# Seven of eight chunks of the experts' gate and up as split products, the down weights' high part in a place of its own

## The chip, the core and the metric

The kernel runs as one program on one core of a Trainium2 chip. The metric is the device time of one execution in microseconds (us); lower is better. The five engines are named as in the profile: PE (TensorE, matrix products; PEld is its weight load), DVE (VectorE), ACT (ScalarE), POOL (GpSimd) and SP (SyncE, which issues most of the DMA transfers).

## The reference

One inference step of a one-layer decoder for 512 prompt tokens and 8 sample tokens, all in float32: a mixing layer (pooling heads and an RG-LRU recurrence), cross-attention to a memory, and a mixture of experts. The change is in the experts alone. There are 64 routed experts of width 256, each token goes to 8 of them, and a shared expert is added:

```python
def body(acc, blk):
    tok, wt, e = blk
    xb = h_pad[tok]
    a = jax.nn.silu(xb @ w_gate[e]) * (xb @ w_up[e])
    yb = (a @ w_down[e]).astype(jnp.float32) * wt[:, None]
    return acc.at[tok].add(yb), None
```

Each expert has `w_gate` and `w_up` of 1024 x 256 and `w_down` of 256 x 1024, 1 MB each. So one pass over the experts reads 3 MB of weights for each of them, beside the tokens' rows.

## The kernel before

All stages ahead of the experts (mixing, attention, routing, shared expert) are as they were, and the change leaves them alone but for places in memory. After some 440 us the expert loop begins. It works on blocks of 96 slots (`SLOTS`), each with the tokens of one expert; there are 64 blocks in this execution, numbered here from 0. The first four (`step_of_block(0, j, peeled=True)`) are written out; the others run in a hardware loop with four blocks a turn (`RING = 4`).

For block b, in the order of PE's instruction stream (`step_of_block` in the tensor program):

- `slots(b + 2)`: five tiny products (L1868) that turn the routing table into the row numbers of block b + 2.
- `gate_up_whole` (L1933): the contraction over D = 1024 is cut into `KD = 8` chunks of 128. The first `WHOLE_K = 2` chunks are multiplied as whole float32, from the raw weights `WG` and the raw tokens `hX`. One such product of 96 tokens by 512 columns (gate and up side by side) is two MATMUL instructions in the trace, called passes below.
- `gate_up(.., 0)` and `gate_up(.., 1)` (L1920): the other six chunks as split products, three chunks in each half. A number is written as a high part (rounded to the PE's one-pass format fp32r) and a low part (the rest), and a product is high*high + low*high + high*low: three MATMULs a chunk.
- `turn_act(b - 1)` (L1940) turns the activations of the block before.
- `turn(b + 1)` (L1905) turns the gathered tokens of the next block, eight transposes into PSUM `pair[1]`.
- `down(b - 1)` (L1954): the down product of the block before as twelve split MATMULs.

ACT makes the high parts by a cast: `cut_up` (L992) in two halves of 1536 elements for gate and up, `cut_down` (L1027) for the 2048 of down, `turn` (L1017 copies the whole chunks to `hX`, L1018 casts the others to `h_parts`), `at` for the activations; it also does the `silu` (L1013) and scales the result (`down`, L1032). DVE subtracts to get the low parts: `cut_up` (L1455), `cut_down` (L1505), `turn` (L1495), `at` (L1509); it does the `gate` product (L1500) and makes the slots' tables (L1342 to L1351).

SP loads the weights into a ring of four sets. `load_up` for block b + 4 (L600 gate, L601 up) waits until `gate_up` of block b is done; `load_down` (L606) until `down` is done. Both loads of `load_up` count on one semaphore, `wg_in`, and ACT's `cut_up(.., 0)` waits for both. POOL gathers the tokens' rows (L706) and adds the results to `acc_rows` in memory (`scatter`, L715). Before the loop it also writes the shared expert's result to `acc_rows` (L724) from `rows`, five transfers, and waits until they have landed (`sums_landed`).

In memory, the high parts of gate and up have two places in `w_hi` (even and odd blocks), 3072 columns each; the high part of down, `WD_hi`, lies between them, in the same 8192 columns.

Of the kernel before, what the change touches and what calls it, by code (L numbers as in the profile page):

```python
# [28 lines left out]
NTT = len(TILES)  # L29
# [7 lines left out]
FE, KF = 256, 2  # L37
# [7 lines left out]
SLOTS = 96  # L45
WHOLE_K = 2
CUT_K = (KD - WHOLE_K) // 2
CUT = CUT_K * 256
RING = 4
# [173 lines left out]
def trunk(nc, x_prompt, x_sample, state_pool, state_conv, state_h, cache_mem_k, cache_mem_v, mem_prompt, norm_mix,  # L223
# [5 lines left out]
    with ExitStack() as ctx:  # L229
# [7 lines left out]

        with nc.sbuf_tensor("w_hi", [P, 8192], F32R) as w_hi:
            pass
# [23 lines left out]
        with nc.sbuf_tensor("unused_L5", [P, 10872], F32), nc.sbuf_tensor("shared_parts", [P, 2, KF, NT], F32R) as shared_parts:  # L263
            pass
        with nc.sbuf_tensor("unused_L3", [P, 10872], F32), nc.sbuf_tensor("h_parts", [P, 2, 2, CUT_K * SLOTS], F32R) as h_parts:
            pass
# [132 lines left out]
        gath = [view(regL, 8824 + D * j, D) for j in range(PAIR)]  # L399
        hX = view(regL, 12024, WHOLE_K, SLOTS)  # L400
        places = view(regL, 14200, 112)
# [6 lines left out]
        WD_lo = [view(lo_A, 4096, KF, D), view(lo_A, 10240, KF, D), view(lo_B, 4096, KF, D), view(lo_B, 6144, KF, D)]  # L408
        WG_hi = [view(w_hi, 5120, 2, 2, CUT), view(w_hi, 0, 2, 2, CUT)]
        last_hi = view(w_hi, 5120, KF, D)  # L410
        sdw_hi, sdw_lo = WD_lo[3], view(lo_C, 4096, KF, D)
        WD_hi = view(w_hi, 3072, KF, D)

# [330 lines left out]
        def _(a):  # L744
# [242 lines left out]
            def cut_up(r, b, q, half):  # L987

                if half == 0:
                    a.wait_ge(wg_in[r], q * 32 + 32)  # L990
                k0 = WHOLE_K + half * CUT_K
                a.copy(WG_hi[r % 2][:, half], WG[r][:, :, k0 * FE:(k0 + CUT_K) * FE]).then_inc(wg_hi, 1)  # L992

# [81 lines left out]
        def _(v):  # L1075
# [375 lines left out]
            def cut_up(r, b, half):  # L1451
                v.wait_ge(wg_hi, 2 * b + half + 1)
                k0 = WHOLE_K + half * CUT_K
                cols = slice(k0 * FE, (k0 + CUT_K) * FE)
                v.tensor_tensor(WG_lo[r][:, :, cols], WG[r][:, :, cols], WG_hi[r % 2][:, half].bitcast(F32),  # L1455
                                ALU.subtract).then_inc(wg_lo, 1)
# [36 lines left out]
            def turn(b):  # L1493
                v.wait_ge(turned_a, b + 1)
                v.tensor_tensor(h_parts[:, 1], pair[1][:, :, SLOTS:(1 + CUT_K) * SLOTS], h_parts[:, 0].bitcast(F32),  # L1495
                                ALU.subtract).then_inc(turned_d, 1)
# [55 lines left out]
        def _(pe):  # L1552
# [344 lines left out]
            def turn(g, b, q, first=False):  # L1897

                pe.wait_ge(gath_in[g], q * 16 + 16)
                if not first:  # L1900
                    pe.wait_ge(turned_d, b)
                g3 = gath[g].rearrange("p (f k) -> p k f", k=KD)
                for k in range(KD):
                    h, n = (k, 0) if k < WHOLE_K else ((k - WHOLE_K) // CUT_K, 1 + (k - WHOLE_K) % CUT_K)
                    ins = pe.transpose(pair[1][:, h, n * SLOTS:(n + 1) * SLOTS], g3[0:SLOTS, k, :], ident[0:SLOTS, 0:SLOTS])  # L1905
                ins.then_inc(turned, 1)

            def gate_up(r, b, half):

                out = pair[0][0:SLOTS, 0, :].rearrange("p (s f) -> p s f", s=2)  # L1910
                hi = WG_hi[r % 2][:, half].rearrange("p s (k f) -> p s k f", k=CUT_K)
                lo = WG_lo[r].rearrange("p s (k f) -> p s k f", k=KD)
                pe.wait_ge(wg_lo, 2 * b + half + 1)
                if half == 0:
                    pe.wait_ge(turned_d, b + 1)
                for k in range(CUT_K):
                    kk = half * CUT_K + k
                    x_hi, x_lo = (h_parts[:, x, half, k * SLOTS:(k + 1) * SLOTS] for x in range(2))
                    for s, (x, w) in enumerate(((x_hi, hi[:, :, k, :]), (x_lo, hi[:, :, k, :]), (x_hi, lo[:, :, WHOLE_K + kk, :]))):
                        ins = pe.matmul(out, x, w, start=False, stop=half == 1 and k == CUT_K - 1 and s == 2,  # L1920
                                        skip_group_check=True)
                if half == 1:
                    ins.then_inc(gu_made, 1)

            def gate_up_whole(r, b, q, first=False):
# [87 lines left out]
```

## Time and profile before

| | |
|---|---|
| time, three executions | 1109.17, 1110.92, 1112.01 us (median 1110.92) |
| the profiled execution | 1109.17 us, its span 1107.4 us |
| PE busy | 1061.4 us, 96% of the span |
| DVE, ACT, POOL busy | 748.3, 646.5, 262.8 us |
| moved by DMA | 299 MB, 270 GB/s over the span |
| granted TensorE clock | 0.982 of full speed over the execution |

The span is what the profiler saw between the first and the last instruction; 1.8 us of the profiled time lie around it. PE's busy time holds overlapping instructions, so it says that PE is nearly always at work, not that it is at its peak. What a stage is bound by is read from the chain of work and from the waits.

### The profile page before, as it was taken

How to read it: one execution, taken by the hardware profiler on the slowest of the kernel's cores; microseconds unless marked ns; L12 is line 12 of the kernel's file. 1: busy time of each engine (PE TensorE's matmuls, PEld its weight loads, DVE VectorE, ACT ScalarE, POOL GpSimd, SP SyncE). 2: the span in 40 equal slices, each digit the busy share in tenths (PEclk: the TensorE clock that was granted, in tenths of full speed). 3: DMA queues.
4: the chain of work that ended last, by engine and by line, in shares of the span. 5: the costliest groups of instructions: out<-in, count | busy, mean ns of one | idle time of the engine just before them, and what ended most of it. 6: DMA issues, size and time to landing. Idle time of an engine off the chain costs nothing.

```text
span 1107.4 us, 17623 instructions
## 1 busy us (share of the span) xinstructions
PE 1061.4 (96%) x5991; PEld 796.5 (72%) x5991; DVE 748.3 (68%) x1332; ACT 646.5 (58%) x850; POOL 262.8 (24%) x180
## 2 busy tenths in 40 slices
PE   5999999999999999999999999999999999999991
PEld 5999458999669888666667666766667666766660
DVE  4733834633934575787788777887788778887762
ACT  4374343432643313677767776677767776677662
POOL 1001320000000101233333333333333333333321
PEclk8999999999999899999999999999999999999996
DMA  9500336050953525899999999999999999999945
GB/s 300 225 4 31 142 143 229 1 229 27 379 211 157 227 79 192 288 359 375 368 367 369 368 377 363 351 357 357 364 366 369 359 356 358 369 367 374 361 113 172
DMA packets 64342, 299.02 MB, mean 270 GB/s; under 512 B 12591, under 2 KB 15227, under 8 KB 39718
## 3 DMA queue, kind: packets, MB, share of 16 engines
q1 hardware_dynamic: 49102, 261.93, 61.7%
q0 software_dynamic: 15200, 36.55, 13.4%
q8 instruction: 26, 0.43, 0.2%
q14 instruction: 14, 0.11, 0.0%
HBM read 281.34 MB, written 34.00 MB: 285 GB/s over the span
## 4 chain that ended last, share of the span: by engine, by line
PE 90%; DMA 3%; DVE 3%; ACT 2%; SPq 1%; issue 1%; POOLq 0%; ACTq 0%; DVEq 0%
PE pair L1920 23%; PE pair L181 18%; PE pair L1954 16%; PE pair L1933 10%; PE pair L1659 5%; PE pair L1905 5%; PE pair L1562 3%; PE pair L1940 1%; DMA regA<-in_w_in 1%; PE pS L1868 1%; PE pair L1752 1%; PE pair L1760 1%; PE pS L1731 1%; DMA acc_rows<-regL 1%; DMA regL<-h_rows,regL 1%; DVE regL L1113 1%
## 5 line engine op out<-in xcount | busy, mean ns | idle before, releaser
L1920 PE MATMUL pair<-w_hi,h_parts 128*96 128x512 f32 x768 | 267.7, 430 | 0.0
L715 POOL DMA_INDIRECT acc_rows<-regL x64 | 93.0, 1453 | 389.8 <-ACT regL L1032 275.2
L1920 PEld LDWEIGHTS pair<-w_hi,h_parts 128*96 128x96 f32 x768 | 121.5, 165 | 69.7 <-issue 33.9
L1954 PE MATMUL pair<-w_hi,act_parts 128*96 128x512 f32 x512 | 165.0, 404 | 2.6 <-DVE act_parts L1509 2.6
L706 POOL DMA_INDIRECT regL<-h_rows,regL x65 | 139.7, 2148 | 74.7 <-DVE regL L1351 49.4
L1032 ACT ACTIVATE regL<-pair,regL 96x1024 f32<-96x1024 f32 x64 | 71.1, 1110 | 125.0 <-PE pair L1954 125.0
L1455 DVE TENSOR_TENSOR lo_A<-regA,w_hi 128x1536 fp32r<-128x1536 f32 x64 | 111.9, 1749 | 0.2 <-ACT w_hi L992 0.2
L1954 PEld LDWEIGHTS pair<-w_hi,act_parts 128*96 128x96 f32 x512 | 80.2, 167 | 29.9 <-issue 2.8
L992 ACT CAST w_hi<-regA 128x1536 fp32r<-128x1536 f32 x64 | 94.7, 1482 | 0.0
L1505 DVE TENSOR_TENSOR lo_B<-regB,w_hi 128x2048 fp32r<-128x2048 f32 x32 | 73.4, 2293 | 29.6 <-ACT w_hi L1027 29.6
L1505 DVE TENSOR_TENSOR lo_A<-regA,w_hi 128x2048 fp32r<-128x2048 f32 x32 | 73.4, 2292 | 24.7 <-ACT w_hi L1027 24.7
L1342 DVE SCALAR_TENSOR_TENSOR regL<-regL 128x480 bf16<-128x480 f32 x66 | 47.4, 719 | 49.3 <-issue 49.3
L181 PE MATMUL pair<-h_hi,win_parts 128*128 128x260 f32 x384 | 71.4, 288 | 5.9 <-DVE h_lo L1107 5.9
L1920 PE MATMUL pair<-lo_A,h_parts 128*96 128x512 f32 x192 | 75.4, 393 | 0.0
L1905 PEld LDWEIGHTS pair<-ident,regL 96*128 96x128 f32 x520 | 67.8, 201 | 8.8 <-DMA regL<-h_rows,regL 1.3
L1905 PE MATMUL pair<-ident,regL 96*128 96x96 f32 x520 | 66.7, 271 | 1.1 <-DMA regL<-h_rows,regL 0.8
L181 PEld LDWEIGHTS pair<-h_hi,win_parts 128*128 128x128 f32 x384 | 60.1, 192 | 6.9 <-issue 5.1
L1933 PE MATMUL pair<-regA,regL 128*96 128x512 f32 x128 | 61.9, 606 | 0.8 <-ACT h_parts L1018 0.8
L1027 ACT CAST w_hi<-regA 128x2048 fp32r<-128x2048 f32 x32 | 60.5, 1891 | 0.0
L1027 ACT CAST w_hi<-regB 128x2048 fp32r<-128x2048 f32 x32 | 60.5, 1890 | 0.0
L1455 DVE TENSOR_TENSOR lo_C<-regC,w_hi 128x1536 fp32r<-128x1536 f32 x32 | 56.0, 1749 | 0.0
L1455 DVE TENSOR_TENSOR lo_B<-regB,w_hi 128x1536 fp32r<-128x1536 f32 x32 | 55.9, 1748 | 0.0
(344 smaller groups left out, 2207.3 us busy)
## 6 DMA issues: line engine op xcount, KB each, us to landing
regA<-in_exp_w_gate SPq DMA_DIRECT2D x32, 1024.0 KB, 9.1
regA<-in_exp_w_up SPq DMA_DIRECT2D x32, 1024.0 KB, 12.2
regA<-in_exp_w_down SPq DMA_DIRECT2D x32, 1024.0 KB, 14.0
regB<-in_exp_w_down SPq DMA_DIRECT2D x32, 1024.0 KB, 15.3
regB<-in_exp_w_gate SPq DMA_DIRECT2D x16, 1024.0 KB, 10.0
regB<-in_exp_w_up SPq DMA_DIRECT2D x16, 1024.0 KB, 13.6
regC<-in_exp_w_gate SPq DMA_DIRECT2D x16, 1024.0 KB, 9.2
regC<-in_exp_w_up SPq DMA_DIRECT2D x16, 1024.0 KB, 12.6
```

Of the source, the lines that this page charges most:

```text
L181: ins = pe.matmul(pair[p][:, h, 0:HALF], w, x[:, k, cols], start=u % 2 == 0 and j == 0 and i == 0, stop=u % 2 == 1 and j == HALF_K - 1 and ...
L706: pool.indirect_dma_start(gath[g][0:SLOTS, :], None, h_rows, bass.IndirectOffsetOnAxis(ap=sums[0:SLOTS, r, 0:1].bitcast(U32), axis=0), bou ...
L715: pool.indirect_dma_start(acc_rows, bass.IndirectOffsetOnAxis(ap=kept[0:SLOTS, r, 0:1].bitcast(U32), axis=0), yX[r][0:SLOTS, :], None, bou ...
L992: a.copy(WG_hi[r % 2][:, half], WG[r][:, :, k0 * FE:(k0 + CUT_K) * FE]).then_inc(wg_hi, 1)
L1027: a.copy(hi, WD[r]).then_inc(wd_hi, 1)
L1032: a.activation(yX[r][0:SLOTS, :].rearrange("p (h n) -> p h n", h=2), pair[2][0:SLOTS, :, :], ACT.Copy, scale=kept[0:SLOTS, r, 1:2]).then_i ...
L1455: v.tensor_tensor(WG_lo[r][:, :, cols], WG[r][:, :, cols], WG_hi[r % 2][:, half].bitcast(F32), ALU.subtract).then_inc(wg_lo, 1)
L1505: v.tensor_tensor(WD_lo[r], WD[r], hi.bitcast(F32), ALU.subtract).then_inc(wd_lo, 1)
L1905: ins = pe.transpose(pair[1][:, h, n * SLOTS:(n + 1) * SLOTS], g3[0:SLOTS, k, :], ident[0:SLOTS, 0:SLOTS])
L1920: ins = pe.matmul(out, x, w, start=False, stop=half == 1 and k == CUT_K - 1 and s == 2, skip_group_check=True)
L1933: pe.matmul(pair[0][0:SLOTS, 0, :].rearrange("p (s f) -> p s f", s=2), hX[:, k, :], w[:, :, k, :], start=k == 0, stop=False, skip_group_ch ...
L1954: ins = pe.matmul(pair[2][0:SLOTS, h, :], act_parts[:, x, k, :], w[:, k, cols], start=k == 0 and s == 0, stop=k == KF - 1 and s == 2)
```

## The change

`WHOLE_K` goes from 2 to 1: one chunk is multiplied whole, seven are split. The halves become three chunks (1 to 3) and four chunks (4 to 7). The high parts of seven chunks need 3584 columns for each of the two places, and `w_hi` grows to 8320 columns that these two fill; the down weights' high part `WD_hi` moves to `wd_parts`, a place over the first part of the region that holds `rows` before the loop. So that the transfers which still read `rows` are done before ACT writes there, ACT now waits for `sums_landed` once, ahead of its step for block 1.

```diff
-WHOLE_K = 2
-CUT_K = (KD - WHOLE_K) // 2
-CUT = CUT_K * 256
+WHOLE_K = 1
+CUT_KS = (range(WHOLE_K, KD // 2), range(KD // 2, KD))
+CUT = (KD - WHOLE_K) * 256
...
-        with nc.sbuf_tensor("w_hi", [P, 8192], F32R) as w_hi:
+        with nc.sbuf_tensor("w_hi", [P, 8320], F32R) as w_hi:
...
+        with nc.sbuf_tensor("unused_L4", [P, 4160], F32), nc.sbuf_tensor("wd_parts", [P, KF * D], F32R) as wd_parts:
...
-        WD_hi = view(w_hi, 3072, KF, D)
+        WD_hi = view(wd_parts, 0, KF, D)
...
-                a.copy(hX[:, :, :], pair[1][:, :, 0:SLOTS])
-                a.copy(h_parts[:, 0], pair[1][:, :, SLOTS:(1 + CUT_K) * SLOTS]).then_inc(turned_a, 1)
+                a.copy(hX, pair[1][:, 0, 0:SLOTS])
+                a.copy(h_parts[:, 0], pair[1][:, :, 0:KD // 2 * SLOTS]).then_inc(turned_a, 1)
...
             for t in range(NTT):
                 start_sums(t)
+            a.wait_ge(sums_landed, 16 * NTT)
...
-                for k in range(CUT_K):
-                    kk = half * CUT_K + k
+                for k in CUT_KS[half]:
+                    n = k % (KD // 2)
```

On PE, in the products of the first block, the kernel before has two whole products ahead of its split ones (`regA` and `regL` are raw weights and raw tokens, `w_hi` the weights' high part, `lo_A` their low part):

```order
L1933 MATMUL pair<-regA,regL 96x512 [waits turned_a,wg_in0]
L1933 MATMUL pair<-regA,regL 96x512
L1920 MATMUL pair<-w_hi,h_parts 96x512 [waits turned_d,wg_lo]
L1920 MATMUL pair<-w_hi,h_parts 96x512
L1920 MATMUL pair<-lo_A,h_parts 96x512
```

and the same place of the change:

```order
L1936 MATMUL pair<-regA,regL 96x512 [waits turned_a,wg_in0]
L1923 MATMUL pair<-w_hi,h_parts 96x512 [waits turned_d,wg_lo]
L1923 MATMUL pair<-w_hi,h_parts 96x512
L1923 MATMUL pair<-lo_A,h_parts 96x512
L1923 MATMUL pair<-w_hi,h_parts 96x512 x2
```

One whole product a block has gone, and the split ones wait for the tokens' low part (`turned_d`) one product sooner; three split products more stand at the end of the second half (12 in place of 9). On ACT, at the entry of the loop (the copies of the shared expert's rows, then block 1), the kernel before has:

```order
L1002 COPY regL<-pair 128x1024 [waits made] x4
L1002 COPY regL<-pair 8x1024 [waits made]
L992 CAST w_hi<-regA 128x1536 [waits wg_in1]
L992 CAST w_hi<-regA 128x1536
L1013 ACTIVATE regL<-pair 96x256 [waits gu_made]
L1017 COPY regL<-pair 128x192 [waits turned]
L1018 CAST h_parts<-pair 128x576
L1027 CAST w_hi<-regA 128x2048 [waits wd_in0]
```

and the change:

```order
L1004 COPY regL<-pair 128x1024 [waits made] x4
L1004 COPY regL<-pair 8x1024 [waits made]
L994 CAST w_hi<-regA 128x2x768 [waits wg_in1,sums_landed]
L994 CAST w_hi<-regA 128x2x1024
L1015 ACTIVATE regL<-pair 96x256 [waits gu_made]
L1019 COPY regL<-pair 128x96 [waits turned]
L1020 CAST h_parts<-pair 128x768
L1029 CAST wd_parts<-regA 128x2048 [waits wd_in0]
```

The order of the instructions is the same; the cast for block 1 now stands behind the landing of the rows, the second cast is a third longer, and so is the cast of the tokens. On DVE, in the step of one block, the kernel before has:

```order
L1505 TENSOR_TENSOR lo_A<-regA,w_hi 128x2048 [waits wd_hi]
L1509 TENSOR_TENSOR act_parts<-pair,act_parts 128x192 [waits at_hi]
L1455 TENSOR_TENSOR lo_B<-regB,w_hi 128x2x768 [waits wg_hi]
L1500 TENSOR_TENSOR regL<-regL,pair 96x256 [waits silu_b]
L1455 TENSOR_TENSOR lo_B<-regB,w_hi 128x2x768 [waits wg_hi]
L1495 TENSOR_TENSOR h_parts<-pair,h_parts 128x576 [waits turned_a]
```

and the change:

```order
L1508 TENSOR_TENSOR lo_A<-regA,wd_parts 128x2048 [waits wd_hi]
L1512 TENSOR_TENSOR act_parts<-pair,act_parts 128x192 [waits at_hi]
L1457 TENSOR_TENSOR lo_B<-regB,w_hi 128x2x768 [waits wg_hi]
L1503 TENSOR_TENSOR regL<-regL,pair 96x256 [waits silu_b]
L1457 TENSOR_TENSOR lo_B<-regB,w_hi 128x2x1024 [waits wg_hi]
L1498 TENSOR_TENSOR h_parts<-pair,h_parts 128x768 [waits turned_a]
```

Nothing has changed places; the last two subtractions are a third longer.

## Rows read from the trace of the kernel before

**Rows 1.** The page: engines' busy time, then the chain's shares.

```profile
PE 1061.4 (96%) x5991; PEld 796.5 (72%) x5991; DVE 748.3 (68%) x1332; ACT 646.5 (58%) x850; POOL 262.8 (24%) x180
...
PE 90%; DMA 3%; DVE 3%; ACT 2%; SPq 1%; issue 1%; POOLq 0%; ACTq 0%; DVEq 0%
```

**Rows 2.** Chain of work, from 690 us: start, us, what.

```profile
689.97 1.29 PE pair L1933 x3
691.25 2.07 PE pair L1920 x9
...
699.43 1.80 PE pair L1933 x4
701.23 0.46 PE pair L1920 x2
```

**Rows 3.** Stretches: engines' busy us (instructions), clock, DMA share, GB/s.

```profile
480.00:680.00 200.00, 200.00 (x983) 137.40 (x983) 161.77 (x222) 144.53 (x161) 73.45 (x40) 1.00 1.02 370
680.00:780.00 100.00, 100.00 (x492) 68.57 (x491) 80.72 (x110) 72.27 (x81) 36.45 (x20) 1.00 1.02 357
...
880.00:980.00 100.00, 100.00 (x493) 68.68 (x491) 80.96 (x111) 72.28 (x81) 36.52 (x20) 1.00 1.02 360
...
610.00:620.00 10.00, 10.00 (x51) 6.87 (x50) 8.10 (x12) 7.22 (x9) 3.68 (x2) 1.00 1.00 349
...
680.00:690.00 10.00, 10.00 (x50) 6.86 (x49) 8.07 (x11) 7.23 (x9) 3.65 (x2) 1.00 0.99 357
```

**Rows 4.** DMA issues at 676, 965 and 1035 us: last column us to landing.

```profile
regC<-in_exp_w_up SPq DMA_DIRECT2D x1, 1024.0 KB, 8.2
...
regA<-in_exp_w_up SPq DMA_DIRECT2D x1, 1024.0 KB, 25.6
...
regC<-in_exp_w_up SPq DMA_DIRECT2D x1, 1024.0 KB, 24.7
```

**Rows 5.** Timeline and chain of block 63's load, casts and products.

```profile
1035.29 0.38 SPq L601 DMA_DIRECT2D regC<-in_exp_w_up  x1
...
1061.12 1.49 ACT L992 CAST w_hi<-regC 128x1536 fp32r<-128x1536 f32 x1
...
1064.65 0.38 ACT L1013 ACTIVATE regL<-pair 96x256 f32<-96x256 f32 x1 [0.38 <-PE pair L1920]
...
1069.31 1.89 ACT L1027 CAST w_hi<-regB 128x2048 fp32r<-128x2048 f32 x1
...
1068.44 1.80 PE pair L1933 x4
```

**Rows 6.** Timeline of DVE in one block.

```profile
702.22 2.29 DVE L1505 TENSOR_TENSOR lo_A<-regA,w_hi 128x2048 fp32r<-128x2048 f32 x1 [0.80 <-ACT w_hi L1027]
...
706.36 0.41 DVE L1500 TENSOR_TENSOR regL<-regL,pair 96x256 f32<-96x256 f32 x1
706.69 1.75 DVE L1455 TENSOR_TENSOR lo_C<-regC,w_hi 128x1536 fp32r<-128x1536 f32 x1
708.36 0.75 DVE L1495 TENSOR_TENSOR h_parts<-pair,h_parts 128x576 fp32r<-128x576 f32 x1
709.44 0.16 DVE L1348 TENSOR_REDUCE regL<-pS 96x2 f32<-96x6 f32 x1 [0.33 <-PE pS L1868]
```

**Rows 7.** Timelines of ACT, POOL and PE where the loop begins.

```profile
441.71 2.85 ACT L992 CAST w_hi<-regA 128x1536 fp32r<-128x1536 f32 x2
...
447.42 1.04 POOL L706 DMA_INDIRECT regL<-h_rows,regL  x1 [4.80 <-DMA acc_rows<-regL]
...
459.94 1.94 PE L1933 MATMUL pair<-regB,regL 128*96 128x512 f32 x4
```

**Rows 8.** SP's issues after the loop's start, and the first one's landing.

```profile
460.07 0.33 SPq L606 DMA_DIRECT2D regA<-in_exp_w_down  x1
466.39 0.33 SPq L600 DMA_DIRECT2D regB<-in_exp_w_gate  x1
...
regA<-in_exp_w_down SPq DMA_DIRECT2D x1, 1024.0 KB, 6.3
```

More of the change, by code:

```diff
@@ L264, in trunk @@
             pass
-        with nc.sbuf_tensor("unused_L3", [P, 10872], F32), nc.sbuf_tensor("h_parts", [P, 2, 2, CUT_K * SLOTS], F32R) as h_parts:
+        with nc.sbuf_tensor("unused_L4", [P, 4160], F32), nc.sbuf_tensor("wd_parts", [P, KF * D], F32R) as wd_parts:
+            pass
+        with nc.sbuf_tensor("unused_L3", [P, 10872], F32), nc.sbuf_tensor("h_parts", [P, 2, 2, KD // 2 * SLOTS], F32R) as h_parts:
             pass
@@ L399, in trunk @@
         gath = [view(regL, 8824 + D * j, D) for j in range(PAIR)]
-        hX = view(regL, 12024, WHOLE_K, SLOTS)
+        hX = view(regL, 12408, SLOTS)
         places = view(regL, 14200, 112)
@@ L408, in trunk @@
         WD_lo = [view(lo_A, 4096, KF, D), view(lo_A, 10240, KF, D), view(lo_B, 4096, KF, D), view(lo_B, 6144, KF, D)]
-        WG_hi = [view(w_hi, 5120, 2, 2, CUT), view(w_hi, 0, 2, 2, CUT)]
-        last_hi = view(w_hi, 5120, KF, D)
+        WG_hi = [view(w_hi, 4160, 2, CUT), view(w_hi, 0, 2, CUT)]
+        last_hi = view(w_hi, 4160, KF, D)
         sdw_hi, sdw_lo = WD_lo[3], view(lo_C, 4096, KF, D)
-        WD_hi = view(w_hi, 3072, KF, D)
+        WD_hi = view(wd_parts, 0, KF, D)
         yf = view(regA, 0, NTT, D)
@@ L990, in cut_up @@
                     a.wait_ge(wg_in[r], q * 32 + 32)
-                k0 = WHOLE_K + half * CUT_K
-                a.copy(WG_hi[r % 2][:, half], WG[r][:, :, k0 * FE:(k0 + CUT_K) * FE]).then_inc(wg_hi, 1)
+                lo, hi = CUT_KS[half][0] * FE, (CUT_KS[half][-1] + 1) * FE
+                a.copy(WG_hi[r % 2][:, :, lo - WHOLE_K * FE:hi - WHOLE_K * FE], WG[r][:, :, lo:hi]).then_inc(wg_hi, 1)
             for half in range(2):
@@ L1452, in cut_up @@
                 v.wait_ge(wg_hi, 2 * b + half + 1)
-                k0 = WHOLE_K + half * CUT_K
-                cols = slice(k0 * FE, (k0 + CUT_K) * FE)
-                v.tensor_tensor(WG_lo[r][:, :, cols], WG[r][:, :, cols], WG_hi[r % 2][:, half].bitcast(F32),
+                lo, hi = CUT_KS[half][0] * FE, (CUT_KS[half][-1] + 1) * FE
+                v.tensor_tensor(WG_lo[r][:, :, lo:hi], WG[r][:, :, lo:hi],
+                                WG_hi[r % 2][:, :, lo - WHOLE_K * FE:hi - WHOLE_K * FE].bitcast(F32),
                                 ALU.subtract).then_inc(wg_lo, 1)
@@ L1494, in turn @@
                 v.wait_ge(turned_a, b + 1)
-                v.tensor_tensor(h_parts[:, 1], pair[1][:, :, SLOTS:(1 + CUT_K) * SLOTS], h_parts[:, 0].bitcast(F32),
+                v.tensor_tensor(h_parts[:, 1], pair[1][:, :, 0:KD // 2 * SLOTS], h_parts[:, 0].bitcast(F32),
                                 ALU.subtract).then_inc(turned_d, 1)
@@ L1903, in turn @@
                 for k in range(KD):
-                    h, n = (k, 0) if k < WHOLE_K else ((k - WHOLE_K) // CUT_K, 1 + (k - WHOLE_K) % CUT_K)
+                    h, n = k // (KD // 2), k % (KD // 2)
                     ins = pe.transpose(pair[1][:, h, n * SLOTS:(n + 1) * SLOTS], g3[0:SLOTS, k, :], ident[0:SLOTS, 0:SLOTS])
@@ L1910, in gate_up @@
                 out = pair[0][0:SLOTS, 0, :].rearrange("p (s f) -> p s f", s=2)
-                hi = WG_hi[r % 2][:, half].rearrange("p s (k f) -> p s k f", k=CUT_K)
+                hi = WG_hi[r % 2].rearrange("p s (k f) -> p s k f", k=KD - WHOLE_K)
                 lo = WG_lo[r].rearrange("p s (k f) -> p s k f", k=KD)
@@ L1915, in gate_up @@
                     pe.wait_ge(turned_d, b + 1)
-                for k in range(CUT_K):
-                    kk = half * CUT_K + k
-                    x_hi, x_lo = (h_parts[:, x, half, k * SLOTS:(k + 1) * SLOTS] for x in range(2))
-                    for s, (x, w) in enumerate(((x_hi, hi[:, :, k, :]), (x_lo, hi[:, :, k, :]), (x_hi, lo[:, :, WHOLE_K + kk, :]))):
-                        ins = pe.matmul(out, x, w, start=False, stop=half == 1 and k == CUT_K - 1 and s == 2,
+                for k in CUT_KS[half]:
+                    n = k % (KD // 2)
+                    x_hi, x_lo = (h_parts[:, x, half, n * SLOTS:(n + 1) * SLOTS] for x in range(2))
+                    for s, (x, w) in enumerate(((x_hi, hi[:, :, k - WHOLE_K, :]), (x_lo, hi[:, :, k - WHOLE_K, :]), (x_hi, lo[:, :, k, :]))):
+                        ins = pe.matmul(out, x, w, start=False, stop=k == KD - 1 and s == 2,
                                         skip_group_check=True)
@@ L1932, in gate_up_whole @@
                 for k in range(WHOLE_K):
-                    pe.matmul(pair[0][0:SLOTS, 0, :].rearrange("p (s f) -> p s f", s=2), hX[:, k, :], w[:, :, k, :],
+                    pe.matmul(pair[0][0:SLOTS, 0, :].rearrange("p (s f) -> p s f", s=2), hX, w[:, :, k, :],
                               start=k == 0, stop=False, skip_group_check=True)
```

## The prediction, made before the change was run

> **What bounds the kernel now.** I read the page first: PE is busy 96% of the span and the chain that ended last runs through PE for 90% of it [rows 1]. That makes PE the bound of the average, so the next view is the chain inside the expert loop, where the change lies. There it is PE alone: from the first split product of one block (691.25 us) to that of the next (701.23) are 9.98 us without a gap [rows 2], and the stretches show PE busy for all of their time [rows 3]. So a PE that does less per block gains at once, if nothing else is as near to its limit. Two things are.
>
> The first is DMA. In the same stretches the mean share of the 16 engines is 1.02, which means that transfers lie one over the other the whole time, and what they move is 370 GB/s up to 680 us, then 357 and 360 [rows 3]. A block needs what 370 GB/s brought in 9.98 us while the loads kept up: 3.69 MB. At 357 to 360 GB/s that takes 10.25 to 10.34 us, longer than PE's block. The landings show it: the last load of a set landed 8.2 us after its issue at 676 us, and 25.6 us after it at 965 us [rows 4]. That is 17.4 us lost over 29 blocks, 0.6 us a block for the slowest of the engines that share a load. PE does not feel it before the end only because the ring of four sets is a reserve, and this reserve is spent: block 63's up weights are issued at 1035.29 and land 24.7 us later, at 1059.99 [rows 4, 5]; ACT's cast of them starts at 1061.12, 1.13 us after that [rows 5].
>
> The second is DVE, whose idle time in a block is 0.80 us before the down weights' subtraction and 0.33 us before the next block's first slot instruction [rows 6], beside an issue gap that stays.
>
> **The change, part by part.** *PE.* Three whole passes take 1.29 us, so one is 0.43 and a chunk (two) 0.86; nine split products take 2.07 us, so one is 0.23 and a chunk (three) 0.69 [rows 2]. A block gets 0.86 - 0.69 = 0.17 us shorter, 9.81 us; for 64 blocks that is 10.9 us.
>
> *ACT and DVE.* The second cast of a block goes from 1.49 to 1.89 us (the down cast has 2048 elements, as it will have) [rows 5]; its subtraction goes from 1.75 to 2.29 us, and the tokens' subtraction from 0.75 to about 0.95 us (576 to 768 elements, at the (2.29 - 1.75)/512 ns per element of the other) [rows 6]. On DVE that is 0.74 us more and a period 0.17 us shorter, 0.91 us, against 1.13 us of waits. It fits with 0.2 us to spare and is costed at nothing. If that cover went, every 0.1 us over would cost 6 us in 62 blocks. ACT's 0.6 us more is of no account; its busy share is 58% [rows 1].
>
> *The wait for the rows, once.* ACT starts the casts for block 1 at 441.71 now. The transfers for which it will wait release POOL's gather at 447.42 [rows 7], so the casts start at about 447.4. Behind the wait stand, on ACT, both casts (1.49 + 1.89) and the silu (0.38) [rows 5], then on DVE the gate (0.41), the longer subtraction (2.29) and the tokens' (0.95) [rows 6]: 7.4 us, and block 1's split products can start at 454.8. The rest of that block is 9.81 - 0.86 = 8.95 us, so block 2 begins at 463.7 where it begins at 459.94 now [rows 7]: 3.8 us later. (PE loses some of that now, in waits at the same place; they are inside the 459.94.)
>
> *The new place of the down weights' high part* costs no instruction; its casts and products keep their sizes. *The smaller copy to hX* is shorter and hidden.
>
> *Where the 0.17 us a block goes.* A faster PE asks for 3.69 MB in 9.81 us, 376 GB/s, more than any long stretch shows [rows 3]. The loads can't come faster, so in the last part of the loop PE waits for them, and the end is set by when block 63's weights land, not by PE's sum. That landing moves only with idle time of the DMA engines. Some comes in at the start: at 466.39 SP issues block 6's loads, and the one before it (issued at 460.07, landed 6.3 us later) lands at 466.4 [rows 8]. There was nothing in stock, so issues that come 3.8 us later leave the engines idle by up to 3.8 us, and all later landings shift by it. Some is won back: the share falls below 1.02 at a few places, 1.00 at 610 us and 0.99 at 680 [rows 3], where a PE ahead of its old pace would have loads waiting; two such stretches hold 0.5 us of idle time, and a few more may add up to 2 us. I call the shift s; its bounds are 0 and 3.8, and I take 2.
>
> From the landing to block 63's first split product the chain is now 1070.24 - 1061.12 = 9.1 us long (1068.44 + 1.80 is that product's start) [rows 5], because PE is late, not ACT. When the loads are late it shrinks to its work: casts and silu 1.49 + 1.89 + 0.38, then 0.41 + 2.29 + 0.95 on DVE, 7.4 us as above. Behind it the second half has three products more, 0.69 us. So the end moves by s - 1.13 - (9.1 - 7.4) + 0.69 = s - 2.1: with s = 2 by -0.1 us, with the bounds by -2.1 to +1.7. Against the profiled execution's 1109.17 (span 1107.4 and 1.8 around it) that is 1109.1, bounds 1107.1 to 1110.9.
>
> The profiled execution is the lowest of three, the others took 1110.92 and 1112.01. PE never waited in the loop of the one that is shown, so I think that in the others late loads had already used up the 1.13 us and the compressible part of the 9.1. By the shorter pieces of now (1.49 twice, 0.38, 0.41, 1.75, 0.75) the chain's least is 6.3 us. In such an execution the change adds s + (7.4 - 6.3) + 0.69 = s + 1.8: 3.8 us with s = 2, bounds 1.8 and 5.6. On 1110.92 that is 1114.7. That the spread comes from there is a guess, so I take a value between the two sums (1109.1 and 1114.7), 1111.5 us: no change that a measurement could tell. For this kernel three executions lie within 0.3%, which I take as about what can be told from no change: below 1107.6 is faster, above 1114.3 slower.
>
> Here two figures of the Trainium skill stand against each other. "DMA: Bandwidth & Descriptors" (Specifications) gives about 358 GB/s of HBM per core, and the late stretches' 357 and 360 agree; by it alone 3.69 MB would take 10.3 us, and this is the forecast. "HBM Reference" (Specifications) says that a core streaming alone measures about 425 GB/s, by which the set would take 8.7 us (an estimate from that page) and DMA would leave PE free; no stretch here shows it beside the gathers and the scatters.
>
> **The rivals.** *PE stays the bound to the end.* Block 2 starts 3.8 us late and 62 blocks win 0.17 each: 3.8 - 10.5 = -6.7, or 1102.5 us against the profiled execution, 1104 against the median. For it speaks that up to 680 us the loads kept pace at 370 GB/s with landings of 8.2 us [rows 3, 4], so that the slow stretches might be a chance of this execution; against it, that they make up most of the loop's second half, and that even 370 is under 376.
>
> *The start's delay is paid in full and nothing is won back (the other side).* The place is ACT's wait at 441.71. With s = 3.8 and loads that bind already, +5.6 us: 1116.5. It decides from s = 1.5 on, where s + 1.8 passes the 3.3 us that can be told. For it: no stock of loads at 466 us [rows 8]. Against it: the profiled execution had 1.13 us and 1.7 us of slack before it.
>
> *DVE becomes the bound.* If its 0.2 us of reserve is not there (a hand-over between ACT and DVE that the sum leaves out), the loop's period is its own, 9.9 or 10 us. As the loads already ask for 10.1 or more in the second half, this adds little to the forecast and would only take away the first rival's gain. It is counted with the forecast.
>
> **How the numbers follow.** Chances: the forecast (loads bind, the start costs some, times of 1107 to 1114.5) 0.60; PE the bound, 1102 to 1105, 0.17; the delay in full, 1114.5 to 1117, 0.23. The range takes in the forecast, the upper half of the first rival and most of the second: 1104 to 1116.5. Faster 0.18, same 0.58, slower 0.24 come from these, with a little of the forecast beyond each bound.
>
> **What would show it.** PE's block in the middle of the loop is 9.81 us (wrong if it is 9.98: a step on DVE or the products is mispriced). Block 2 starts near 463.7, with ACT's cast for block 1 near 447.4 behind the landing of the rows. In the loop's second half PE shows gaps that ACT's first cast ends, with DMA named as what is waited for, and block 63's up weights land within 2 us of 1062. The share of DMA stays at 1.02 and the rate at 355 to 370 GB/s. The prediction is wrong if the rate rises to 376 with PE's share at full to the end (the first rival), or if DVE has no idle time left before 680 us.

## The result, and the profile after

The changed kernel takes 1132.68 us (median of four, 1127.46 to 1136.80) against 1110.05 (1108.87 to 1112.01): a ratio of 1.0195, with a 95% interval of 1.0171 to 1.0219. The forecast was 1111.5 in a range of 1104 to 1116.5, so it was 21 us off, and the time lies above the range's upper end. Ratios in this document leave out executions that are over 1.5% above the fastest of the same kernel, so for a kernel whose times spread they differ from the ratio of the medians.

The profiled execution has 1132.45 us and a span of 1130.7. Its page, to be put beside [rows 1]:

```profile
PE 1064.8 (94%) x6055; PEld 804.2 (71%) x6055; DVE 792.2 (70%) x1332; ACT 667.6 (59%) x850; POOL 262.6 (23%) x180
...
DMA 49%; PE 40%; issue 4%; DVE 3%; ACT 2%; SPq 1%; POOLq 1%; POOL 0%; ACTq 0%; DVEq 0%
```

PE's busy time hardly moved, and DVE's grew by 44 us, about what its longer subtractions ask for; but the chain that ended last is another: PE's 90% of it became 40%, and 49% is DMA now. In the loop that chain is one kind of transfer after another (start, us, what):

```profile
591.98 10.10 DMA acc_rows<-regL
...
602.97 8.98 DMA acc_rows<-regL
...
612.87 9.74 DMA acc_rows<-regL
...
623.50 9.24 DMA acc_rows<-regL
```

These are the scatters that add a block's result to `acc_rows`. Each must wait until the one ahead has landed (`sums_landed`), and none of the eight groups of rows ahead of the prediction looks at them. The waits from 480 to 1080 us (total, times, longest) say the same, and that PE now waits for the gathered tokens:

```profile
POOL acc_rows L717 <- DMA acc_rows<-regL: 358.3, 56, 6.9
...
PEld pair L1908 <- DMA regL<-h_rows,regL: 36.2, 45, 1.6
...
PE pair L1908 <- DMA regL<-h_rows,regL: 17.5, 29, 1.2
```

Over the same stretch of the kernel before, the scatter's longest wait is for its own sums:

```profile
POOL acc_rows L715 <- ACT regL L1032: 245.6, 41, 6.0
```

The stretches that answer to [rows 3]:

```profile
480.00:680.00 200.00, 194.53 (x977) 135.57 (x976) 171.36 (x214) 146.64 (x158) 74.02 (x39) 1.00 1.02 358
680.00:780.00 100.00, 97.03 (x483) 66.58 (x481) 84.32 (x109) 73.24 (x77) 34.21 (x19) 1.00 1.02 354
880.00:980.00 100.00, 95.82 (x480) 66.45 (x479) 83.78 (x106) 72.78 (x79) 35.57 (x20) 1.00 1.02 353
```

PE is no longer busy all the time. The DMA share is 1.02 as before at a lower rate, and yet the loads are in good time: block 63's up weights are issued at 1061.19, land 10.6 us later and are cast at 1086.97, 15 us after that (in [rows 5] the slack was 1.13 us). The timeline, then the DMA issue with its us to landing:

```profile
1061.19 0.38 SPq L603 DMA_DIRECT2D regC<-in_exp_w_up  x1
...
1086.97 1.48 ACT L994 CAST w_hi<-regC 128x1536 fp32r<-128x1536 f32 x1
```

```profile
regC<-in_exp_w_up SPq DMA_DIRECT2D x1, 1024.0 KB, 10.6
```

The 23.3 us that the span grew by add up so, from the starts of the whole product: block 2 begins at 466.30 instead of 459.94 (6.4 us); from there to block 63 are 627.7 us instead of 608.4 (19.3 us, 10.29 us a block against 9.97); and the end behind it is 36.7 us long instead of 39.1 (-2.4).

**Why a scatter takes longer.** The timelines of POOL and of DVE's down subtraction, in the kernel before and then in the change:

```profile
601.68 1.45 POOL L715 DMA_INDIRECT acc_rows<-regL  x1 [6.01 <-issue]
603.43 2.21 POOL L706 DMA_INDIRECT regL<-h_rows,regL  x1 [0.31 <-issue]
611.62 1.45 POOL L715 DMA_INDIRECT acc_rows<-regL  x1 [5.98 <-ACT regL L1032]
...
602.49 2.29 DVE L1505 TENSOR_TENSOR lo_B<-regB,w_hi 128x2048 fp32r<-128x2048 f32 x1 [0.81 <-ACT w_hi L1027]
...
612.45 2.29 DVE L1505 TENSOR_TENSOR lo_A<-regA,w_hi 128x2048 fp32r<-128x2048 f32 x1 [0.79 <-ACT w_hi L1027]
```

```profile
602.97 1.95 POOL L717 DMA_INDIRECT acc_rows<-regL  x1 [6.41 <-DMA acc_rows<-regL]
605.23 1.16 POOL L708 DMA_INDIRECT regL<-h_rows,regL  x1 [0.30 <-issue]
612.87 3.02 POOL L717 DMA_INDIRECT acc_rows<-regL  x1 [6.48 <-DMA acc_rows<-regL]
616.20 1.16 POOL L708 DMA_INDIRECT regL<-h_rows,regL  x1 [0.30 <-issue]
...
601.31 2.29 DVE L1508 TENSOR_TENSOR lo_B<-regB,wd_parts 128x2048 fp32r<-128x2048 f32 x1 [0.35 <-ACT wd_parts L1029]
...
612.28 2.29 DVE L1508 TENSOR_TENSOR lo_B<-regB,wd_parts 128x2048 fp32r<-128x2048 f32 x1 [0.80 <-ACT wd_parts L1029]
```

Before, the scatter starts 1.0 us after ACT has the sums and 0.8 us ahead of DVE's subtraction, and takes 1.45 us on POOL. After, it starts during the subtraction. The first one ends at 604.92, 1.32 us after the subtraction's end (603.60); the second at 615.89, 1.32 us after 614.57. In the change 57 of the 64 scatters start during a down subtraction, and all 57 end 1.31 to 1.34 us behind its end; the other seven take 1.42 to 1.76 us. So the scatter's instruction is held by DVE's; `down_pieces4` below puts that to the test.

The subtraction is as long before as after, and the hold was there before too, on the gather: the one at 603.43 starts during the subtraction and takes 2.21 us where the change's take 1.16. In the kernel before 61 of the 65 gathers start so, and all end 0.85 to 0.88 us behind the subtraction's end. PE never waited in these stretches [rows 3], so it cost nothing; in the change the scatter has taken the gather's place.

From its end to its landing a scatter needs about 6.9 us, before (6.85, mean of blocks 4 to 30) as after (6.90). A round of the chain is then 0.89 us (the shortest time from a landing to the next start) + 2.56 (mean on POOL) + 6.9 = 10.35 us; measured 10.34.

The Trainium skill, in "SBUF — State Buffer" (SBUF: two separate sides), names a trap of this kind: while VectorE runs an operation in a two-port mode, a float32 copy for example, GpSimd can't write the descriptors of a transfer from its queue, which then waits until the operation ends instead of being slowed in proportion. By the same page of the Trainium skill (Who interferes with whom) an operation with two inputs, such as this subtraction, has no two-port mode; it gets in the way of what GpSimd reads from SBUF, and where it was tried it didn't stall a transfer. Here it did, 57 times of 57: the wait until the end agrees with the trap, its condition doesn't, and the measurement decides. Whether it matters that the row numbers of these transfers lie in SBUF, no run here shows. The 1.32 us behind the end are this case's number.

The next gather stands behind the scatter in POOL's queue. Behind the one at 602.97 it starts at 605.23 and lands about 10 us later, when PE stands ready to turn the tokens. PE's block is 9.86 us where nothing is waited for (609.34 to 619.20), but the next gather sets the pace.

```profile
609.34 1.08 PE L1936 MATMUL pair<-regA,regL 128*96 128x512 f32 x2
...
619.20 1.08 PE L1936 MATMUL pair<-regA,regL 128*96 128x512 f32 x2
```

### The profile page after: what moved, and what is told of

Same layout as the page of the kernel before. It is cut to its first block, busy times and chain, and to the rows that moved or that the text cites. A ratio compares the mean times of both kernels' runs of the same rounds, so it can differ in the third digit from the quotient of the medians.

```text
span 1130.7 us, 17752 instructions
## 1 busy us (share of the span) xinstructions
PE 1064.8 (94%) x6055; PEld 804.2 (71%) x6055; DVE 792.2 (70%) x1332; ACT 667.6 (59%) x850; POOL 262.6 (23%) x180
## 4 chain that ended last, share of the span: by engine, by line
DMA 49%; PE 40%; issue 4%; DVE 3%; ACT 2%; SPq 1%; POOLq 1%; POOL 0%; ACTq 0%; DVEq 0%
DMA acc_rows<-regL 46%; PE pair L181 18%; PE pair L1662 5%; PE pair L1923 3%; PE pair L1565 3%; PE pair L1957 2%; DMA regA<-in_w_in 1%; PE pair L1755 1%; PE pair L1763 1%; PE pS L1734 1%; DMA regL<-h_rows,regL 1%; DVE regL L1116 1%; PE pair L1908 1%; PE pair L1800 1%; PE pair L1832 1%
## 5 line engine op out<-in xcount | busy, mean ns | idle before, releaser
L717 POOL DMA_INDIRECT acc_rows<-regL x64 | 152.6, 2384 | 409.8 <-DMA acc_rows<-regL 362.6
L1957 PE MATMUL pair<-wd_parts,act_parts 128*96 128x512 f32 x504 | 160.9, 400 | 0.0
L708 POOL DMA_INDIRECT regL<-h_rows,regL x65 | 79.9, 1229 | 78.0 <-DVE regL L1354 52.8
L1957 PEld LDWEIGHTS pair<-wd_parts,act_parts 128*96 128x96 f32 x504 | 78.5, 166 | 26.5
L1508 DVE TENSOR_TENSOR lo_A<-regA,wd_parts 128x2048 fp32r<-128x2048 f32 x32 | 73.3, 2292 | 19.8 <-ACT wd_parts L1029 19.8
L1508 DVE TENSOR_TENSOR lo_B<-regB,wd_parts 128x2048 fp32r<-128x2048 f32 x31 | 71.0, 2292 | 20.0 <-ACT wd_parts L1029 20.0
L1457 DVE TENSOR_TENSOR lo_B<-regB,w_hi 128x1536 fp32r<-128x1536 f32 (+1 forms) x32 | 64.5, 2014 | 0.0
L1457 DVE TENSOR_TENSOR lo_C<-regC,w_hi 128x1536 fp32r<-128x1536 f32 (+1 forms) x32 | 64.5, 2014 | 0.0
L1498 DVE TENSOR_TENSOR h_parts<-pair,h_parts 128x768 fp32r<-128x768 f32 x64 | 60.6, 947 | 1.6 <-ACT h_parts L1020 1.6
L1029 ACT CAST wd_parts<-regA 128x2048 fp32r<-128x2048 f32 x32 | 60.7, 1896 | 0.0
## 6 DMA issues: line engine op xcount, KB each, us to landing
regB<-in_exp_w_up SPq DMA_DIRECT2D x16, 1024.0 KB, 11.3
```

What stands on the lines that cost most here:

```text
L708: pool.indirect_dma_start(gath[g][0:SLOTS, :], None, h_rows, bass.IndirectOffsetOnAxis(ap=sums[0:SLOTS, r, 0:1].bitcast(U32), axis=0), bou ...
L717: pool.indirect_dma_start(acc_rows, bass.IndirectOffsetOnAxis(ap=kept[0:SLOTS, r, 0:1].bitcast(U32), axis=0), yX[r][0:SLOTS, :], None, bou ...
L1029: a.copy(hi, WD[r]).then_inc(wd_hi, 1)
L1457: v.tensor_tensor(WG_lo[r][:, :, lo:hi], WG[r][:, :, lo:hi], WG_hi[r % 2][:, :, lo - WHOLE_K * FE:hi - WHOLE_K * FE].bitcast(F32), ALU.sub ...
L1498: v.tensor_tensor(h_parts[:, 1], pair[1][:, :, 0:KD // 2 * SLOTS], h_parts[:, 0].bitcast(F32), ALU.subtract).then_inc(turned_d, 1)
L1508: v.tensor_tensor(WD_lo[r], WD[r], hi.bitcast(F32), ALU.subtract).then_inc(wd_lo, 1)
```

## The experiments

Four questions were put. Is it the chain of scatters, and by which part does it reach PE? Does the subtraction's length set the hold? Does the late start matter beyond its own delay? And where are the loads, on which the forecast rested?

### Two accumulators, and the gather ahead of the scatter

`two_sums` gives odd blocks an accumulator of their own, so a scatter waits only for the last but one; at the end both are read and added.

```diff
-                pool.wait_ge(sums_landed, b * 16 + 16 * NTT)
+                odd, of_kind = j % 2, turn * (RING // 2) + (j - j % 2) // 2
+                pool.wait_ge(odd_landed if odd else sums_landed, of_kind * 16 + 16 * NTT)
```

> The changed kernel with two sums in memory, one for even and one for odd blocks, so that a result's scatter-add waits for the landing of the one before the last and no longer of the last; the two are added at the end. Theory A (the chain of scatter-adds, each behind the landing of the one before, sets the pace of 10.3 us a block): the chain falls apart, PE's block is 9.83 us, at most 10.0 where loads bind, and the time is 1104 to 1114 us with some 4 us for the second sum at the end. Theory B (the 16 DMA engines are full at 355 GB/s and the scatter-adds are late only for that): the block stays at 10.2 to 10.4 us, the time at 1128 to 1138 us, and PE waits for weights in place of gathered rows.

1128.13 us (1127.62 to 1130.26), ratio 1.0150 (1.0130 to 1.0170). By its time alone theory B was right and theory A missed by 14 us. The blocks say the opposite, here two starts of the whole product in the chain of work:

```profile
602.74 0.94 PE pair L1948 x2
...
612.59 0.94 PE pair L1948 x2
```

The block is 9.85 us up to block 32, where casts begin to wait for loads, and block 63 begins at 1077.06, 17 us sooner than in the change. What takes that back is the reading and adding of two sums at the end: behind block 63 come 48.8 us instead of 36.7, 12 us more where theory A reckoned with 4. So the chain was the cause of the 10.3 us a block.

`gather_first` keeps one accumulator and puts each scatter one step later in POOL's order, so that a gather stands behind the scatter of a block that is one older:

```diff
-                if not (peeled and j < 2):
-                    scatter((j - 2) % RING, b - 2)
+                if not (peeled and j < 3):
+                    scatter((j - 3) % RING, b - 3)
```

> The changed kernel with each scatter-add moved one block later in POOL's order, so that the gather for which PE waits stands ahead of it. Theory A: the chain of scatter-adds is not shortened, PE runs ahead by what the ring of results allows and then keeps its pace of 10.3 us a block; the time is 1126 to 1136 us. Theory C (only the gather's place behind a late scatter-add costs the time): PE's block is 9.83 us, the time 1104 to 1114 us.

1112.26 us (1110.12 to 1119.20), ratio 1.0016 (0.9995 to 1.0036): 20 us of the loss are gone with the serial chain still there. In blocks 4 to 30 a scatter comes every 10.08 us, and the blocks every 9.85; so the scatters fall behind their sums, from 1.9 us at block 0 to 8.4 at block 30, and the ring of four places for the results takes that up. So over these blocks the chain costs PE time only through the gather that stands behind it, as theory C says. The waits from 880 to 1080 us show what is next:

```profile
POOL acc_rows L717 <- DMA acc_rows<-regL: 115.7, 18, 7.1
...
ACT w_hi L994 <- DMA regA<-in_exp_w_up: 10.0, 9, 1.7
...
ACT w_hi L994 <- DMA regC<-in_exp_w_up: 4.7, 4, 1.7
```

From block 45's on ACT's casts wait for the up weights, which land 26 to 29 us after their issue; PE waits for no gathered tokens there. This is the bound that the prediction named, and it appears once the gather is out of the way.

### The length of the hold

`down_pieces4` is the change with the down subtraction cut in four, 0.68 us each:

```diff
-                v.tensor_tensor(WD_lo[r], WD[r], hi.bitcast(F32), ALU.subtract).then_inc(wd_lo, 1)
+                for k in range(KF):
+                    for at0 in range(0, D, 512):
+                        cols = slice(at0, at0 + 512)
+                        v.tensor_tensor(WD_lo[r][:, k, cols], WD[r][:, k, cols], hi[:, k, cols].bitcast(F32), ALU.subtract).then_inc(wd_lo, 1)
```

> The changed kernel with DVE's subtraction for the down weights (2.29 us, 2048 elements) cut into four of 512. Theory A with the hold (POOL's scatter-add can't write its descriptors while that subtraction runs, which makes it 2.4 us long in place of 1.45 and keeps the chain late): POOL's scatter-add falls to 1.5 to 1.9 us, the block to 9.85 to 10.0 us, the time to 1106 to 1118 us. If the 2.4 us have another cause: scatter-add and block as in the changed kernel, the time 1130 to 1140 us, DVE being some 0.2 us longer in each block.

1115.44 us (1110.46 to 1120.83), ratio 1.0034 (1.0007 to 1.0062). The scatter takes 1.67 us (mean of blocks 4 to 30) instead of 2.56, and starts 1.2 us after its sums instead of 2.9:

```profile
605.75 1.82 POOL L717 DMA_INDIRECT acc_rows<-regL  x1 [6.88 <-DVE regL L1354]
607.87 1.44 POOL L708 DMA_INDIRECT regL<-h_rows,regL  x1 [0.30 <-issue]
615.77 1.66 POOL L717 DMA_INDIRECT acc_rows<-regL  x1 [6.46 <-DMA acc_rows<-regL]
...
606.56 2.50 DVE L1511 TENSOR_TENSOR lo_B<-regB,wd_parts 128x512 fp32r<-128x512 f32 x4 [0.16 <-ACT wd_parts L1029]
```

A scatter comes every 9.94 us, as the blocks do, and casts wait for loads from block 35's on. (Its times lie in two groups, five up to 1112.60 and five from 1118.28, which is the profiled one; why is not known.) DVE's work is not less, the four pieces take 2.50 us together where one took 2.29; only the piece that can hold POOL is shorter, and 17 us came back.

### The place and its start wait

`place_alone` is the kernel before with only the new place of the down weights' high part and the wait for `sums_landed` that it needs.

```diff
-        WD_hi = view(w_hi, 3072, KF, D)
+        WD_hi = view(wd_parts, 0, KF, D)
...
+            a.wait_ge(sums_landed, 16 * NTT)
```

> The kernel before with the new place of the down weights' high part and the one wait for it, and no other change. Theory A: PE's block stays at 9.98 us, the scatter-adds' chain (9.6 us) doesn't bind, and the start of the loop costs 3 to 6 us: 1112 to 1117 us. Theory D (the new place or the late start is what makes the loop slow): a block of 10.2 us or more, 1124 to 1136 us.

1116.16 us (1108.68 to 1128.64), ratio 1.0031 (1.0010 to 1.0052). In the profiled execution the scatters are not held (1.45 us) and block 2 starts 3.8 us late, at 463.72; casts wait for loads from block 34's on. Two of the ten times, 1127.42 and 1128.64, lie 8.6 us or more above all the others; neither was profiled, so whether scatters were held in them, at 9.97 us a block, is open.

Three runs move that wait from before block 1's casts to where the place is first written:

```diff
-            a.wait_ge(sums_landed, 16 * NTT)
...
+                if peeled and j == 1:
+                    a.wait_ge(sums_landed, 16 * NTT)
                 cut_down((j - 1) % RING, b - 1, landed)
```

`place_late` does it to `place_alone`:

> The kernel before with the down weights' high part in a place of its own, as place_alone (1116.2 us), but the wait for the rows stores moved to just before the down cast of block 0. Block 2 started at 463.7 us in place_alone; here by 461. If the late start is what cost place_alone its 5 us (theory S): 1109.5 to 1113. If it is the other effect of the place, that the loads' landings fall behind from block 10 on instead of block 30 on (theory L, whatever the start): 1114.5 to 1118.

1108.92 us (1107.41 to 1113.36), ratio 0.9990 (0.9974 to 1.0006), block 2 at 459.58. That is 0.6 us below theory S's range. Against `place_alone` the medians differ by 7.2 us, the ratios by 0.41%, some 4.6 us, and block 2 comes 4.1 us sooner; so the late start, not the place, was most of the cost. Whether there is more is open.

`late_wait` does it to the change:

> The changed kernel with nothing but ScalarE's start wait moved to just before the down cast of block 0; the scatter still stands ahead of the gather and the subtraction is whole. Theory A1 (the scatter of every block is caught by the subtraction once blocks come every 9.83 us, however the loop begins: 0.89 hand-over + 9.45 landing = 10.34 us a block): only the start's 3 to 4 us come back, 1126 to 1130, and each scatter starts 0.89 us after the landing ahead. Theory A2 (there are two regimes: a scatter that starts 1.0 us after its sums is 0.8 us ahead of the subtraction, takes 1.45 us and lands after 8.7, so 9.6 us a block fit into 9.83; one that is late by more than 0.8 us is caught, and stays caught; in the changed kernel the late start makes the first ones late): 1108 to 1116, blocks of 9.85 us for at least the first part of the loop.

Its twelve times lie in two groups, six from 1111.22 to 1114.91 and six from 1126.42 to 1131.33, with none between (median 1120.67, ratio 1.0060, 1.0024 to 1.0096, the ratio resting on eight of the twelve). The median lies in neither theory's range; the lower group lies in that of A2, and the upper reaches from that of A1 to above it. The profiled execution (1114.02) shows both regimes in one loop:

```profile
522.10 3.27 POOL L717 DMA_INDIRECT acc_rows<-regL  x1 [7.03 <-DMA acc_rows<-regL]
...
533.37 1.90 POOL L717 DMA_INDIRECT acc_rows<-regL  x1 [6.52 <-DMA acc_rows<-regL]
...
543.66 3.10 POOL L717 DMA_INDIRECT acc_rows<-regL  x1 [6.93 <-DMA acc_rows<-regL]
...
613.95 1.45 POOL L717 DMA_INDIRECT acc_rows<-regL  x1 [6.07 <-DMA acc_rows<-regL]
...
623.60 1.63 POOL L717 DMA_INDIRECT acc_rows<-regL  x1 [5.87 <-DMA acc_rows<-regL]
...
521.76 2.29 DVE L1509 TENSOR_TENSOR lo_B<-regB,wd_parts 128x2048 fp32r<-128x2048 f32 x1 [0.36 <-ACT wd_parts L1029]
...
614.58 2.29 DVE L1509 TENSOR_TENSOR lo_A<-regA,wd_parts 128x2048 fp32r<-128x2048 f32 x1 [0.34 <-ACT wd_parts L1029]
```

From 522 to 576 us the scatters start during the subtraction and come 10.2 to 11.3 us apart. One at 584.75 starts 0.28 us ahead of it; from then on they take 1.45 to 1.65 us, and PE's block is 9.85 until loads bind at block 38. So the two regimes of theory A2 are there in one loop, each feeding itself for several blocks, since a held scatter lands late and makes the next one late. The start wait is not needed for the held one. That half of these executions were in it for most of the loop is inferred from their times; none of them was profiled. The start wait may make it likelier, as all four times of the change lie above 1127; but four are few, and what first makes a scatter late is not shown.

`gather_late` puts the late wait and the gather ahead of the scatter together:

> The changed kernel with the gather ahead of the scatter (as in gather_first, 1112.3 us) and with ScalarE's new wait for the four rows stores moved from before block 1's casts to just before the down cast of block 0. Block 2 started at 464.3 us in gather_first and at 459.9 in the kernel before; with the wait moved it should start by 461. Theory S (the start wait is paid in full at the end): 1107.5 to 1110. Theory L (from about block 44 on the landing of the loads sets the pace, and they can't be had sooner): the 3 to 4 us are used up as a longer queue at the casts, 1110.5 to 1114.

1107.95 us (1105.71 to 1110.28), ratio 0.9977 (0.9963 to 0.9990): 0.2% faster than the kernel before, with an interval that lies just below 1, and 4.3 us under `gather_first`. So the start's delay is paid in full at the end, theory S: block 2 begins at 460.68, 3.6 us sooner than in `gather_first`, and block 63 at 1067.15, 1.2 us sooner than in the kernel before.

`gather_before` is the control, the kernel before with the gather ahead:

> The kernel before with the gather ahead of the scatter in GpSimd's queue and nothing else changed. Theory A: there the scatter waits for its sums and not for the scatter ahead, and its start doesn't hold the gather long enough to reach TensorE (2 us of slack at the turn), so the order is worth nothing: 1109 to 1113, blocks of 9.97 us. If the gather's place were worth something by itself, without the longer scatter: below 1107.

1109.71 us (1107.12 to 1110.81), ratio 0.9995 (0.9983 to 1.0008), blocks of 9.97 us. The order is worth nothing by itself, as theory A said, but not for its reason: 43 of the 64 scatters start during a down subtraction, nearly all wait for the one ahead, and in blocks 4 to 30 they come 10.06 us apart. So a held chain needs no shorter block; here too it falls behind, and no gather is late for it.

`gather_late_pieces` adds the four pieces of `down_pieces4` to `gather_late`:

> gather_late (1107.95 us) with VectorE's down subtraction in four pieces of 512 columns. Theory L (with the gather ahead, the landing of the loads sets the pace of the last third, and the scatters have the ring's slack): no change, 1106 to 1110. If the scatters still cost something there through their hold: 1103 to 1106.

1106.28 us (1104.09 to 1109.34), ratio 0.9965 (0.9950 to 0.9980), the lowest median here. It lies at the border of the two ranges, so the time decides nothing between them. Its block is 9.93 us to the end, because DVE has become the bound: its down subtraction waits 0.20 us for ACT's cast in `gather_late`, and next to never here, where its pieces take 0.2 us more. The row of `gather_late`, then that of this run:

```profile
601.53 2.29 DVE L1509 TENSOR_TENSOR lo_B<-regB,wd_parts 128x2048 fp32r<-128x2048 f32 x1 [0.20 <-ACT wd_parts L1029]
```

```profile
603.49 2.50 DVE L1512 TENSOR_TENSOR lo_B<-regB,wd_parts 128x512 fp32r<-128x512 f32 x4
```

In the profiled execution no cast waits for a load and PE is busy from 840 to 1040 us, so the loads do not set its pace, although they are near: from block 50 on the up weights are cast 0.7 to 1.9 us after their landing. That block 63 begins at 1067.6, about where it does in `gather_late` with its faster blocks and its waits for loads, is no proof of theory L.

### The loads

`gather_light` is `gather_first` with a sixth fewer bytes of weights; it leaves out the second half of the down product:

```diff
-                sp.dma_start(WD[r][:, :, :], ed[bass.ds(e, 1)].rearrange("e p k d -> p (e k) d")).then_inc(wd_in[r], 16)
+                sp.dma_start(WD[r][:, 0:1, :], ed[bass.ds(e, 1), :, 0:1, :].rearrange("e p k d -> p (e k) d")).then_inc(wd_in[r], 16)
...
-                a.copy(hi, WD[r]).then_inc(wd_hi, 1)
+                a.copy(hi, WD[r][:, 0:1, :].to_broadcast([P, KF, D])).then_inc(wd_hi, 1)
```

> gather_first with only the first of the two halves of the down weights loaded for the blocks from 4 on (0.52 MB of 3.15 MB of weights a block less), the cast reads that half twice, and the subtraction is two instructions of half the size: the second half of the down product is left out of the reckoning, so it isn't the reference's product. Theory L (in gather_first the loads' landing set the pace from block 44 on, at 1112.3 us): with a sixth fewer bytes the block stays at 9.85 us to the end, block 63 starts at 464.3 + 61 x 9.85 = 1065 and the kernel ends at 1103 to 1106. If it is the late scatters or something else on the engines that lengthens the blocks there: 1110 to 1114, with casts that wait for nothing.

1107.63 us (1105.36 to 1109.80), ratio 0.9968 (0.9956 to 0.9981); the profiled execution took 1109.5. `gather_first` from 840 to 1040 us, then this run from 800 to 1040:

```profile
840.00:1040.00 200.00, 196.25 (x988) 137.18 (x987) 175.45 (x217) 149.42 (x159) 57.26 (x39) 1.00 1.02 364
```

```profile
800.00:1040.00 240.00, 240.00 (x1220) 168.66 (x1219) 217.72 (x292) 182.33 (x195) 79.67 (x48) 1.00 0.96 319
```

PE is busy throughout, the block stays at 9.87 us to the end, and in this stretch the up weights land 8 to 12 us after their issue. With fewer loads a scatter also needs only 4.6 us from its instruction's end to its landing instead of 7.2, and the scatters no longer fall behind; so the run takes the late scatters away together with the late loads, and by itself doesn't tell one from the other. What tells them apart are the waits in `gather_first`: casts wait for loads, and PE for no tokens. So the loads did bind there, and theory L is right on that. Its time was missed by 1.6 us: this profiled execution reaches block 2 3.1 us later than the one it was reckoned from (467.39 for 464.27). The last scatter of each run, behind which no loads are left, lands 2.5 to 3.1 us after its instruction's end; so more than half of the 7.2 us goes with the other transfers.

## Why the prediction was wrong, step by step

**PE's block, 9.81 us: right.** Where PE waits for nothing the block is 9.83 to 9.86 us.

**"Two things are" as near to their limit as PE, DMA and DVE: the step that failed.** A third was as near, POOL's chain of scatters, and it entered the sum at nothing, without a look: of POOL the prediction has one gather at the loop's start [rows 7]. The chain's shortest round is 0.89 + 8.3 to 8.9 us (means from start to landing, 8.3 in the kernel before, 8.86 in `place_alone`), 9.2 to 9.75. At 9.83 us a block that leaves little or no slack, a scatter that is 0.8 us late falls into the 2.29 us subtraction, the round becomes 10.34, and the gather behind it is late for PE. That is 19 of the 23 us. `two_sums`, `down_pieces4` and `gather_first` each remove it in their own way.

**DVE's longer subtractions, costed at nothing: right for DVE's time.** The lengths were right (2.28 for 2.29, 0.95 for 0.95 us), and so was the reserve of 0.2 us: it is the 0.20 us of wait in `gather_late`, and with 0.2 us more DVE became the bound. But the prediction asked only whether DVE has the time, not whom its instructions hold; and the one that holds the scatter, the down subtraction, the change didn't touch.

**The wait for the rows: right in its first half, short in its second.** The cast for block 1 came at 447.51 (worked out: 447.4), its split products at 454.73 (454.8). Block 2 came at 466.30 instead of 463.7, because "the rest of that block" took 11.57 us, not 8.95. The timeline of PE, then two stretches of 5 us:

```profile
451.99 1.07 PE L1936 MATMUL pair<-regA,regL 128*96 128x512 f32 x2 [3.06 <-ACT h_parts L1020]
454.73 1.14 PE L1923 MATMUL pair<-w_hi,h_parts 128*96 128x512 f32 x2 [1.67 <-DVE h_parts L1498]
```

```profile
450.00:455.00 5.00, 1.34 (x3) 0.55 (x4) 4.48 (x6) 5.00 (x6) 0.00 (x0) 0.87 1.01 392
455.00:460.00 5.00, 5.00 (x14) 3.30 (x14) 3.50 (x6) 0.84 (x3) 1.36 (x1) 0.50 0.30 84
```

PE waited 3.06 and 1.67 us there, and was then granted 0.50 of its clock (1.2 GHz) from 455 to 460 us. In those 5 us it did the work of 2.5 at the upper level (2.4 GHz), about the 2.6 us that were missing. That start costs its delay in full, as the second rival said: 4.3 us between `gather_first` and `gather_late`.

**Loads that bind in the second half: the mechanism right, but hidden.** At 10.3 us a block they had 15 us of slack. In `gather_first` it shows as described, and with fewer loads, in `gather_light`, it is gone. A size was off a little: 364 and 366 GB/s went through late in the loop of `gather_first` and `gather_late` (840 to 1040 us), not 357 to 360. Reading saturation from the share of 1.02 was wrong: the change has 1.02 at 353 to 358 GB/s with loads in time, `gather_first` 1.02 at 364 with loads late. The landing times tell them apart, the share doesn't. Of the two figures that the prediction cites from the Trainium skill, 358 GB/s ("DMA: Bandwidth & Descriptors", Specifications) and 425 ("HBM Reference", Specifications), the rates of these stretches beside gathers and scatters, 353 to 370, lie by the first.

**The rivals.** PE as the bound to the end (1102.5 to 1104) was reached by no run's median. The delay in full (1116.5) described only 4 to 6 of the 23 us. A rival for the queue that PE's next tokens come through was missing, and so was any sum above 1116.5.

## What to carry to other kernels

Before a change that makes blocks shorter, list every serial chain that runs once a block, those of transfers too, and set each one's round beside the new block, not only the chain that ends last now. Ask of each longer instruction also what it holds: in these runs a VectorE subtraction of 2.29 us held a GpSimd transfer's issue, and pieces of 0.68 us held it less. Put the transfer that the next block needs ahead of the one that may be late.

## What was not expected of the hardware

- A scatter-add issued by GpSimd that starts during VectorE's two-input float32 subtraction ends 1.32 us behind the subtraction's end (57 of 57 in the change, 1.31 to 1.34); by itself its instruction takes 1.45 us. A gather is held in the same way, to 0.85 to 0.88 us behind the end (61 of 61 in the kernel before). Four scatters of other runs that start 0.01 to 0.04 us into the subtraction are not held (1.46 to 1.53 us); one that starts 0.05 us into it is.
- Serial scatter-adds of 96 rows: 0.89 us from a landing to the next start at the least, then 6.9 to 7.4 us from the instruction's end to the landing (means of blocks 4 to 30) where 353 to 370 GB/s are moved, 4.6 us where it is 320, 2.5 to 3.1 for the last scatter.
- One loop can have two self-feeding paces: in `late_wait` scatters 10.2 to 11.3 us apart and then 9.6 to 9.9. Its times, 1111 to 1115 and 1126 to 1131 us, suggest that executions differ in how long they stay in each. What tips the loop into one was not settled, nor why the loads' landings begin to lag at block 10 in `place_alone` and only at block 30 in the kernel before, at the same pace.
- Behind two waits of 3.06 and 1.67 us PE's granted clock was 0.50 from 455 to 460 us; in `gather_late`, behind waits of 0.89 and 1.08 us at the same place, it was 1.00.
